# A ring of sixteen weight buffers in place of twelve, and experts in pairs in two loops

## The reference, cut to what matters

```python
cap = max(1, EC_CAPACITY_FACTOR * N // N_EXPERTS)          # 64 latent, 16 context tokens for each expert
aff = jax.nn.softmax((h @ w_router).astype(jnp.float32), axis=-1)
gates, idx = lax.top_k(aff.transpose(0, 2, 1), cap)        # each of 16 experts picks its tokens
def one(hb, gb, ib):
    xe = hb[ib]
    hid = jax.nn.silu(jnp.einsum('ecd,edf->ecf', xe, w_gate)) * jnp.einsum('ecd,edf->ecf', xe, w_up)
    ye = jnp.einsum('ecf,efd->ecd', hid, w_down) * gb[..., None].astype(hb.dtype)
    return jnp.zeros_like(hb).at[ib.reshape(-1)].add(ye.reshape(-1, D))
```

## Time and profile before

| What | Value |
|---|---|
| Median of 3 runs | 1711.03 us (1709.94 to 1712.18) |
| The profiled execution's own time | 1713.24 us |
| Its span | 1711.3 us |
| Granted TensorE clock over the span | 0.989 |
| TensorE busy | 1666.0 us |
| First matmul of expert 0 | 700.50 us |
| Experts 1 to 14, each | 61.99 us |
| Last scatter on GpSimd starts | 1706.08 us |

### The profile page before, as it was taken

How to read it: one execution, slowest core, us unless ns; L and a number is a source line. 1 busy time by engine, 2 the same in 40 slices (tenths; PEclk the granted TensorE clock), 3 DMA queues, 4 the chain that set the end, 5 groups by cost and what they waited for, 6 DMA issues and landing times.

```text
span 1711.3 us, 32043 instructions
## 1 busy us (share of the span) xinstructions
PE 1666.0 (97%) x13900; PEld 859.0 (50%) x13900; DVE 565.0 (33%) x974; ACT 343.3 (20%) x702; POOL 284.9 (17%) x238
## 2 busy tenths in 40 slices
PE   6999999999999989899999999999999999999997
PEld 3767778778888868333333333333333333333332
DVE  2797627347676684311011011011011101101101
ACT  4533222246666733100000000000000000000000
POOL 1364404000010000101210220220220121121011
PEclk9999999999999999899999999999999999999998
DMA  9446644323132044799999999999999999999994
GB/s 337 164 155 213 216 171 136 103 79 97 41 97 79 33 176 158 286 421 412 412 421 414 413 418 417 413 413 422 412 413 422 413 413 421 414 413 421 414 414 168
DMA packets 122198, 507.34 MB, mean 296 GB/s; under 512 B 13100, under 2 KB 35076, under 8 KB 72984
## 3 DMA queue, kind: packets, MB, share of 16 engines
q1 hardware_dynamic: 111856, 484.80, 70.8%
q0 software_dynamic: 9536, 21.52, 4.5%
q10 hardware_dynamic: 744, 0.15, 0.0%
HBM read 487.02 MB, written 19.42 MB: 296 GB/s over the span
## 4 chain that ended last, share of the span: by engine, by line
PE 90%; DVE 3%; DMA 3%; issue 1%; POOL 1%; ACT 1%; SPq 0%; DVEq 0%; ACTq 0%; POOLq 0%
PE banks L2139 56%; PE banks L1761 8%; PE banks L1763 7%; PE banks L1762 7%; PE banks L1991 2%; PE banks L1978 2%; PE banks L1902 2%; DMA raw_k<-in_w_down_e 1%; PE banks L1786 1%; DMA raw<-in_w_ada 1%; PE banks L1805 1%; PE banks L1940 1%; POOL qk_swp L1654 0%; DVE var L1157 0%; PE banks L2088 0%
## 5 line engine op out<-in xcount | busy, mean ns | idle before, releaser
L2139 PE MATMUL banks<-raw,xe 128*32 128x512 f32 x2304 | 255.8, 596 | 2.3 <-DVE xe L1443 2.3
L1610 DVE TENSOR_TENSOR hid<-banks,sg 128x512 f32<-128x512 f32 x48 | 31.1, 673 | 599.9 <-PE banks L2139 599.9
L1761 PE MATMUL banks<-w_hi,h_hi 128*128 128x512 f32 x560 | 225.8, 403 | 3.2 <-DVE w_lo L1090 2.9
L1763 PE MATMUL banks<-w_lo,h_hi 128*128 128x512 f32 x560 | 219.6, 392 | 0.0
L1762 PE MATMUL banks<-w_hi,h_lo 128*128 128x512 f32 x560 | 218.9, 391 | 0.0
L1726 POOL DMA_INDIRECT out<-yeg_c,idx_c x64 | 83.5, 1305 | 811.6 <-DVE yeg_c L1595 797.0
L1069 ACT ACTIVATE sg<-banks 128x512 f32<-128x512 f32 x48 | 25.2, 597 | 904.8 <-PE banks L2139 904.8
L2139 PEld LDWEIGHTS banks<-raw,xe 128*32 128x32 f32 x2304 | 75.0, 111 | 168.8 <-issue 166.2
L2139 PE MATMUL banks<-raw_x,hT 128*32 128x512 f32 (+1 forms) x1536 | 127.4, 486 | 3.4 <-DMA raw_x<-in_w_down_e 3.4
L2139 PE MATMUL banks<-raw_k0.5_54,xe 128*32 128x512 f32 x1152 | 129.8, 592 | 0.0
L2139 PE MATMUL banks<-raw_x,xe 128*32 128x512 f32 x1152 | 126.7, 592 | 0.0
(11 more groups left out here) (249 smaller groups left out, 1899.9 us busy)
## 6 DMA issues: line engine op xcount, KB each, us to landing
raw<-in_w_gate_e SPq DMA_DIRECT2D x48, 1024.0 KB, 20.6
raw<-in_w_up_e SPq DMA_DIRECT2D x48, 1024.0 KB, 21.9
raw_x<-in_w_down_e SPq DMA_DIRECT2D x48, 1024.0 KB
raw_k0.5_54<-in_w_gate_e SPq DMA_DIRECT2D x32, 1024.0 KB, 20.4
raw_k1.5_55<-in_w_gate_e SPq DMA_DIRECT2D x32, 1024.0 KB
raw_x<-in_w_up_e SPq DMA_DIRECT2D x32, 1024.0 KB
raw_k<-in_w_up_e SPq DMA_DIRECT2D x32, 1024.0 KB, 22.1
raw_k1.5_55<-in_w_down_e SPq DMA_DIRECT2D x32, 1024.0 KB
```

Source lines behind the costliest of these rows:

```text
L1610: nc.vector.tensor_tensor(hid[:, part, :].rearrange("p (f a j) -> p f a j", j=STRIP, a=2), in_turn(bank(3 + part)), in_turn(sg[:, part, :] ...
L1761: nc.tensor.matmul(ps, hi, wh, start=first, stop=False)
L1763: return nc.tensor.matmul(ps, hi, wl, start=False, stop=last)
L2139: done = nc.tensor.matmul(out(i), left(i), right(i), start=first, stop=last)
```

## The change

The ring gets four more places, so that `NEX` is 16: two new buffers `raw_w0` and `raw_w1`, laid over `x2` and over `h2T`, and the places `NRAWE + 0` and `NRAWE + 1`, which held weights of the first stage. 24 is no multiple of 16, so an expert starts at place 0 or at place 8, by turns. `slot_of`, `expert_buffer`, `expert_loaded`, `expert_loads` and `expert` take an argument `odd` for it, and both loops take two experts in one pass. Before the experts, chunk 3 is loaded when the stores of `x2` are in, chunks 4 to 7 and 8 to 12 after the two halves of the context's projection, and chunks 13 to 15 when the context's router product is done.

```diff
-NOWN = 8
+NOWN = 10
-EXPERT_SLOT = [2, 0, 1] + [NRAWE + i for i in range(4, 8)] + list(range(NRAW, NRAWE)) + [NRAWE + 2, NRAWE + 3]
+EXPERT_SLOT = [2, 0, 1, NRAWE + 8] + [NRAWE + i for i in range(4, 8)] + list(range(NRAW, NRAWE)) + [NRAWE + i for i in (2, 3, 0, 1, 9)]
...
+    def slot_of(odd, i):
+        return EXPERT_SLOT[(EC * odd + i) % NEX]
+    def expert_buffer(odd, i):
+        return raw_slot(slot_of(odd, i)).rearrange("p a n -> p (a n)")
...
+    raw_w = [place(f"raw_w{i}", [P, CK, CW], offset=offset) for i, offset in enumerate((WORK + 4 * 2 * COLS_X * KT, WORK + 4 * NT * D + 12 * D))]
...
-        def expert_loaded(e, i):
-            slot = EXPERT_SLOT[i % NEX]
-            return raw_in[slot], e * (16 * EC // NEX) + 16 * (RAW_BEFORE[slot] + i // NEX + 1)
+        def expert_loaded(e, odd, i):
+            slot, turn = slot_of(odd, i), (EC * odd + i) // NEX
+            return raw_in[slot], e * (16 * EC // NEX) + (16 * (RAW_BEFORE[slot] + turn + 1) - odd * (16 * EC // NEX))
...
             for t in range(NL):
                 store_tile(t)
+            sp.wait_ge(x2_out, 16 * NL)
+            load_expert(3)
             sp.wait_ge(p2_done, P2.index(("W", NL, 0)) + 1)
-            for i in range(3, 7):
+            for i in range(4, 8):
                 load_expert(i)
             sp.wait_ge(p2_done, P2.index(("W", NL, 1)) + 1)
-            for i in range(7, 10):
+            for i in range(8, NEX - 3):
                 load_expert(i)
             store_tile(NL)
+            sp.wait_ge(p2_done, P2.index(("L", NL, 0)) + 1)
+            for i in range(NEX - 3, NEX):
+                load_expert(i)
             sp.wait_ge(xg_in, 16 * (PARTS_X - 1))
-            for i in range(10, NEX):
-                load_expert(i)
...
-            expert_loads(0, False)
-            with sp.Fori(1, E - 1) as e:
-                expert_loads(e, False)
-            expert_loads(E - 1, True)
+            expert_loads(0, 0, False)
+            with sp.Fori(1, E - 2, 2) as e:
+                expert_loads(e, 1, False)
+                expert_loads(e + 1, 0, False)
+            expert_loads(E - 1, 1, True)
...
-            expert(0, True, False)
-            with pe.Fori(1, E - 1) as e:
-                expert(e, False, False)
-            expert(E - 1, False, True)
+            expert(0, 0, True, False)
+            with pe.Fori(1, E - 2, 2) as e:
+                expert(e, 1, False, False)
+                expert(e + 1, 0, False, False)
+            expert(E - 1, 1, False, True)
```

More of the change, by code:

```diff
@@ L389, in expert_source @@
         return w[e, :, k, :] if isinstance(e, int) else w[bass.ds(e, 1), :, k, :].rearrange("e p n -> p (e n)")
-    def expert_buffer(i):
-        return raw_slot(EXPERT_SLOT[i % NEX]).rearrange("p a n -> p (a n)")
+    def slot_of(odd, i):
+        return EXPERT_SLOT[(EC * odd + i) % NEX]
+    def expert_buffer(odd, i):
+        return raw_slot(slot_of(odd, i)).rearrange("p a n -> p (a n)")
     base = (nc.sbuf_base + 31) // 32 * 32
@@ L550, in trunk_program @@
     xt = place("xt", [P, PARTS_X, KT, STRIP], offset=WORK + 4 * COLS_X * KT)
+    raw_w = [place(f"raw_w{i}", [P, CK, CW], offset=offset) for i, offset in enumerate((WORK + 4 * 2 * COLS_X * KT, WORK + 4 * NT * D + 12 * D))]
     def raw_slot(i):
-        return raw[:, i] if i < NRAW else raw_x[:, i - NRAW] if i < NRAWE else raw_k[(i - NRAWE) // 2][:, i % 2]
+        return raw[:, i] if i < NRAW else raw_x[:, i - NRAW] if i < NRAWE else raw_k[(i - NRAWE) // 2][:, i % 2] if i < NRAWE + 8 else raw_w[i - NRAWE - 8]
     ctx = ExitStack()
@@ L673, in load_expert @@
                 slot = EXPERT_SLOT[i]
-                sp.dma_start(expert_buffer(i), expert_source(0, i)).then_inc(raw_in[slot], 16)
+                sp.dma_start(expert_buffer(0, i), expert_source(0, i)).then_inc(raw_in[slot], 16)
             for t in range(NL):
@@ L766, in _, with expert_loads @@
                 sp.dma_start(gate2_c[STRIP * i:STRIP * i + STRIP, :], gate_d[1, 1:2, c].broadcast_to([STRIP, CW // 2])).then_inc(gate2_in, 16)
-            def expert_loads(e, last):
+            def expert_loads(e, odd, last):
                 for i in range(EC):
@@ L777, in expert_loads @@
                     sp.wait_ge(chunk_read, e * EC + (i + 1))
-                    sp.dma_start(expert_buffer(j % EC), src).then_inc(raw_in[EXPERT_SLOT[j % NEX]], 16)
-            expert_loads(0, False)
-            with sp.Fori(1, E - 1) as e:
-                expert_loads(e, False)
-            expert_loads(E - 1, True)
+                    sp.dma_start(expert_buffer(odd, i), src).then_inc(raw_in[slot_of(odd, i)], 16)
+            expert_loads(0, 0, False)
[3 more added lines that the diff above has]
+            expert_loads(E - 1, 1, True)
         @block.scalar
@@ L2157, in down_latent, with down_rows @@
                                  lambda i: w[:, CW * (i // 2):CW * (i // 2) + CW], f == 0, f == FE // P - 1)
-            def down_rows(f):
-                return expert_buffer(ES + f // 2)[:, D * (f % 2):D * (f % 2) + D]
+            def down_rows(odd, f):
+                return expert_buffer(odd, ES + f // 2)[:, D * (f % 2):D * (f % 2) + D]
             def first_gate():
@@ L2171, in first_gate, with expert @@
                         stage_step(("F", 0))
-                    pe.wait_ge(*expert_loaded(0, i))
+                    pe.wait_ge(*expert_loaded(0, 0, i))
                     for part in range(2):
-                        hidden_part(0, part, i, expert_buffer(i))
+                        hidden_part(0, part, i, expert_buffer(0, i))
                 pe.wait_ge(xec_ready, 1)
                 for i in range(KT):
-                    hidden_part(0, 2, i, expert_buffer(i)).then_inc(chunk_read, 1)
-            def expert(e, first, last_e):
+                    hidden_part(0, 2, i, expert_buffer(0, i)).then_inc(chunk_read, 1)
+            def expert(e, odd, first, last_e):
                 if first:
@@ L2184, in expert @@
                         pe.wait_ge(xe_ready, e * 2 + 2)
-                    pe.wait_ge(*expert_loaded(e, i))
-                    w = expert_buffer(i)
+                    pe.wait_ge(*expert_loaded(e, odd, i))
+                    w = expert_buffer(odd, i)
                     for n, part in enumerate(PARTS):
@@ L2196, in expert @@
                     if f % 2 == 0:
-                        pe.wait_ge(*expert_loaded(e, ES + f // 2))
-                    last = down_context(f, down_rows(f))
+                        pe.wait_ge(*expert_loaded(e, odd, ES + f // 2))
+                    last = down_context(f, down_rows(odd, f))
                 if last_e:
@@ L2203, in expert @@
                     if not last_e and f >= AHEAD and f % 2 == 0:
-                        pe.wait_ge(*expert_loaded(e, ES + f // 2))
-                    last = down_latent(f, down_rows(f))
+                        pe.wait_ge(*expert_loaded(e, odd, ES + f // 2))
+                    last = down_latent(f, down_rows(odd, f))
                     if not last_e:
                         if f >= AHEAD:
-                            last = down_context(f, down_rows(f))
+                            last = down_context(f, down_rows(odd, f))
                         if f % 2 == 1:
```

## The result

The changed kernel takes 1780.31 us (median of 4 runs, 1779.86 to 1780.85) where the kernel before takes 1711.61 in the same comparison: ratio 1.0402, 95% interval 1.0384 to 1.0420. The forecast was 1716.6 with a range up to 1726. It is slower, as forecast, but by twelve times as much. The profiled execution has a span of 1778.7 us (before 1711.3), and its mean granted clock is 0.972 (0.989).

What follows compares the result with a forecast made beforehand. TensorE was taken to bound the loop and weight transfers the last expert. -9.3 (buffers) + 0.5 (loads) + 14.4 (jumps) = +5.6 us on the 1711.03 us median gave 1716.6 us, range 1701.5 to 1726.

Steps and rivals of the forecast that it cites:

- What bounds the kernel: Whole kernel: TensorE sets the pace inside the loop; in the last expert late weight transfers, 2.47 us apart, do.
- Step 3, experts in pairs: TensorE's loop: ten-block body not kept, each of six jumps back stalls 2.4 us; +14.4 us, bounds 0 and 28.
- The rival of the clock: TensorE's jumps: each stall of 3.3 us also costs 1.7 us of clock; +21.2, 1732 us, chance 0.12.
- Step 1, four more buffers: Last expert: transfers asked for four reads earlier, so its waits and slow clock go; -9.3 us, bounds 0 and -9.3.
- Step 2, the loads before the loop: Ahead of the loop: both gathers share queues with the moved loads; +0.5 us, bounds 0 and 3.9.
- Free jumps: TensorE's loop: jumps cost nothing, body kept or fetch hidden by the lead; 1702.2 us, chance 0.21.
- A short fetch: TensorE's jumps: fetch of 2.2 us, 1.0 us per jump, 6 us in all; 1708.2 us, chance 0.20.
- No tail gain: Last expert: extra buffers land after 718, last transfer stays at 1687.9; with the jumps 1726 us, chance 0.05.

Runs made afterwards that it cites:

- Experiment 7: Kernel before, in the last expert the context half reads four buffers, then latent and context buffers by turns; 1702.65 us, ratio 0.9961.
- experiment 4: Changed kernel with the first instruction of TensorE's loop placed at the start of a 16 KB block; 1748.09 us, ratio 1.0225.
- experiment 2: Kernel before with only TensorE's loop taking two experts in one pass, ring of twelve kept; 1777.60 us, ratio 1.0396.
- experiment 1: Changed kernel with TensorE's experts 1 to 14 written out instead of in a loop, ring of sixteen kept; 1715.66 us, ratio 1.0029.
- experiment 12: Kernel before with TensorE's loop over pairs and only 188 of 320 products of an expert left in that loop; 1710.27 us.
- experiment 13: Kernel before with TensorE's loop over pairs and only 146 of 320 products of an expert left in that loop; 1709.24 us.
- experiment 3: Changed kernel with a hint at the top of TensorE's loop that names the target of the jump at its end; 1731.17 us, ratio 1.0119.
- experiment 11: Changed kernel with both the loop's head at the start of a block and the backward jump announced on TensorE; 1725.96 us, ratio 1.0112.
- experiment 9: Kernel before with TensorE's loop over pairs and 272 of 320 products of an expert left in that loop; 1723.06 us, ratio 1.0081.

## Why the prediction was wrong

*What bounds the kernel* was read rightly: TensorE in the loop, the transfers in the last expert. Experiment 7 takes the latter away and gains most of what the waits and the clock of the earlier trace rows had cost (6.6 us of 9.3).

*Step 3, experts in pairs, failed in its size.* The mechanism was named (a body of ten blocks isn't kept, six jumps stop TensorE), and the stops came at the six places as written (with thirteen packets in a pass, not ten). The text had 2.4 us for each jump; measured are 12.6. Three things were missing. First, the fetch itself: I took the 3.5 us of a 4 KB store of the earlier trace rows as the nearest row. The gap is 5.3 us, with some 1.2 us of lead ahead of it, so TensorE goes on about 6.5 us after the branch begins, as the branch's own 6.56 us says; it lies beyond the 5.9 us that I had as the upper end. The block's own transfer was sized rightly (1.05 us; measured 1.0 to 1.8), but some 3.5 us pass from the beginning of the branch until the last block ahead of its end begins to come, and 1.5 us behind it. The row of the store was measured outside a full queue, while here the weights hold the engines at 1.01; no run takes the fetch out of the full queue, so what that adds stays open. Second, the block behind the loop's head, 4.3 us: experiment 4 shows that it comes from where the loop's head lies in its block. I had counted one block for each jump, and no view of the kernel before shows the head's place. Third, the clock, 3.0 us. The rival of the clock had the mechanism and a chance of 0.12, but at 1.7 us, for one gap of 3.3 us. In sum 5.3 + 4.3 + 3.0 = 12.6. The upper bound of 28 us for the six jumps stood in the text; they took 75.8, so the range couldn't hold it. It had no term for more than one fetch to a jump.

The sentence of the Trainium skill (Runtime: NRT & Kernel Launch, Instruction fetch mechanics) that spoke against this part was right in its direction. Its 128 KiB in blocks of 16 KiB would keep eight; here 6.1 packets of 16 KB were kept and 7.2 were not, so this case's bound lies lower. A body that begins inside a block touches one more, which would bring the two closer; that wasn't tried.

*Step 1, four more buffers, was right in its sum by luck, and wrong in its reason.* The last expert is 9.4 us shorter where -9.3 was forecast. But experiment 2 has the same end with twelve buffers, so it came from the stops. "From there the engines do the same work in the same order" was the sentence that failed: without a kept body the code comes over the same engines, 1.05 MB of it in 800 us, and the weights lose 0.7%. In experiment 1 half of the engines have carried all they had by 1676, 8 us ahead of the 1684 of the kernel before, about as the step said (1678.0 for its last buffer); the other half ends some 14 us behind it, and so the last buffer lands 4 us later than before. Its transfer was issued at 1664.18, not four reads earlier but 0.35 us ahead of the 1664.53 of the earlier trace rows, since SP's issues had become slow by then; but in 1600 to 1676 the engines stood at a share of 1.02, so this left none of them without work. The ring's worth without the code's traffic wasn't measured: one expert has 24 chunks, 24 is no multiple of 16, so a body of one expert can't carry a ring of sixteen, and the short pairs of experiments 12 and 13 were run with twelve.

*Step 2, the loads before the loop,* was inside its bounds but not at +0.5: the context's gather is issued at 710.80 and taken up by VectorE at 716.84, 6.0 us instead of the 2.7 of the earlier trace rows, and TensorE waits 1.9 us (2.9 in experiment 1). The DMA share in 706 to 720 is 0.62, twice that of the earlier trace rows, so the queue had not run empty by 711. The gather went through queues that were still in part full: 6.0 us lies near the 6.88 that I had as its price there, and the 2.9 us of experiment 1 are the upper end of what I had for this wait.

*The rivals.* Free jumps fell, though experiment 12 shows that a body of 6.1 packets has them. A short fetch fell. The clock's rival is the one that came nearest, in kind. "No tail gain" fell in the changed kernel and came true in experiment 1.

## What to carry to other kernels

Before a loop's body is made longer, count the packets of instructions in the trace of one pass: a body that fetches nothing is worth keeping, and what lies beyond the bound is fetched whole, in every pass. A price for a stall on a saturated chip is to be taken from rows inside the saturated stretch, and a stall's price is the gap, what follows it, and the clock. Where transfers are late only at the end, look first for work that can be done between them.

## What the runs showed of the hardware

- A taken branch of TensorE to code that isn't kept takes 5.9 to 6.8 us, with the DMA engines full, and 4.1 to 4.5 us where it is announced (experiments 3 and 11); one to kept code takes 0.21 to 0.24.
- The packet of code that such a branch waits for takes 1.0 to 1.8 us. It starts 3.4 to 3.7 us after the beginning of the branch (changed kernel, experiments 4 and 9), and 1.5 to 2.0 us where the jump is announced; the branch ends 1.4 to 1.5 us after it.
- The bound for a loop's body lies between 6.1 and 7.2 packets of 16 KB, and beyond it nothing is kept.
- A stop of 5.0 us is followed by 10 us at a granted clock of 0.50; after stops of 2.8 to 2.9 us the clock fell at three of six jumps (experiment 11).
- With instruction packets at 0.5% of the engines the weights' rate falls by 0.7% (403.9 to 401.1 GB/s), and at the end half of the engines are 14 us behind the others (share 0.51 in 1676 to 1690 of experiment 1).
- SP's issues become slow in experiment 1: 0.33 us each in the loop of the kernel before and in that of the changed kernel, about 2 us there late in the run, and one of 6.09 us at 1544.40. The ring of sixteen alone doesn't do it, since the changed kernel has it too.
